# Two transformer blocks on one Trainium2 core: seven quarter products per weight tile in the first block's output products and in the second block's input product, with modulation weights brought as halves

## The reference

```
for l in range(2):                                       # first block
    shift, scale, gate = split(silu(c) @ w_ada[l] + b_ada[l], 3)
    h = rms_norm(x, norm_w[l]) * (1 + scale) + shift
    mix = three_mixers(h @ w_in[l])
    x = x + gate * (mix @ w_out[l])
sh1, sc1, ga1, sh2, sc2, ga2 = split(silu(c_2) @ w_mod + b_mod, 6)      # second block
px = (rms_norm(x, norm_mix) * (1 + sc1) + sh1) @ w_in_2
pc = (the same of ctx, with its own modulation) @ w_in_2
mix = mixers(px, pc)           # conv3 over tokens of the columns, wkv scans, short conv, Fourier
x = x + ga1 * (mix @ w_out_2)
x = x + ga2 * ((silu(h3 @ w_gate) * (h3 @ w_up)) @ w_down)
out = rms_norm(x, norm_final)
```

## Time and profile of the kernel before

| | before |
|---|---|
| runs | 3432.41, 3434.14, 3436.14 us |
| span of the profiled execution | 3419.8 us |
| its own time | not listed apart from the three runs |
| median of the runs less this span | 14.3 us |
| PE busy | 3148.4 us (92%) |
| DVE, ACT, POOL busy | 1497.6, 543.4, 900.9 us |
| mean granted TensorE clock | 0.963 |
| output products of layer 0 | 593.6 to 709.4 us of the span |
| output products of layer 1 | 1245.4 to 1372.1 us |
| second block's input product | 1379.0 to 1817.9 us |

### The profile page before, as it was taken

One profiled execution on the slowest core, in us unless ns is written; L12 is line 12 of the kernel. 1 busy time (PEld: TensorE's weight loads), 2 busy tenths in 40 slices (PEclk: granted clock), 3 DMA queues, 4 the chain that ended last, 5 costly groups with the idle time before them and its releaser, 6 DMA issues.

```text
span 3419.8 us, 67514 instructions
## 1 busy us (share of the span) xinstructions
PE 3148.4 (92%) x31278; PEld 2723.8 (80%) x31278; DVE 1497.6 (44%) x2300; ACT 543.4 (16%) x1011; POOL 900.9 (26%) x545
## 2 busy tenths in 40 slices
PE   5999999998999999999996888887899999999998
PEld 4877887877878888444785777677889999999998
DVE  4745365464447511333534666667334432113111
ACT  1012102020210211100002344333110000000001
POOL 1000000000000010000000121112447797777774
PEclk8998999998999999999997999999999999999999
DMA  7955387764336553333772000000436654444443
GB/s 275 409 219 197 133 328 280 307 247 172 124 136 255 200 194 123 148 148 141 264 296 112 8 9 10 7 7 6 159 126 232 237 217 162 167 170 161 161 163 109
DMA packets 52571, 582.97 MB, mean 170 GB/s; under 512 B 6931, under 2 KB 9297, under 8 KB 10433
## 3 DMA queue, kind: packets, MB, share of 16 engines
q1 hardware_dynamic: 34352, 465.06, 35.9%
q0 software_dynamic: 17936, 113.59, 8.6%
HBM read 576.52 MB, written 2.10 MB: 169 GB/s over the span
## 4 chain that ended last, share of the span: by engine, by line
PE 75%; DVE 10%; DMA 7%; ACT 3%; issue 3%; POOL 1%; SPq 0%; ACTq 0%; DVEq 0%; POOLq 0%
PE PS L1599 24%; PE PS L366 14%; PE PS L1548 10%; PE PS L664 6%; DMA ring<-in_w_second_dram 3%; DMA ring<-in_w_vec_dram 2%; PE PS L409 2%; PE PS L1767 1%; PE PS L1780 1%; PE PS L363 1%; DVE ring L201 1%; PE PS L1616 1%; DMA ring<-in_w_start_dram 1%; PE PS L1558 1%; PE PS L1812 1%
## 5 line engine op out<-in xcount | busy, mean ns | idle before, releaser
L366 PE MATMUL PS<-H,ring 128*128 128x256 f32 x2944 | 668.8, 386 | 7.0 <-ACT H L694 7.0
L366 PEld LDWEIGHTS PS<-H,ring 128*128 128x128 f32 x2944 | 562.1, 193 | 94.9 <-issue 17.6
L1548 PE MATMUL PS<-H,ring 128*128 128x256 f32 (+2 forms) x1344 | 403.1, 462 | 5.7 <-DMA ring<-in_w_second_dram 5.5
L1599 PE MATMUL PS<-H,ring 128*128 128x128 f32 x3424 | 404.0, 275 | 2.2 <-DMA ring<-in_w_second_dram 2.2
L1599 PEld LDWEIGHTS PS<-H,ring 128*128 128x128 f32 x3424 | 394.2, 192 | 3.0 <-DMA ring<-in_w_second_dram 2.6
L1548 PEld LDWEIGHTS PS<-H,ring 128*128 128x128 f32 (+1 forms) x1344 | 254.1, 190 | 155.0 <-issue 124.7
L2224 DVE TENSOR_TENSOR W<-W,PS 128x256 f32<-128x256 f32 x58 | 24.4, 421 | 679.9 <-ACT W L1925 679.8
L1599 PE MATMUL PS<-H,W 128*128 128x128 f32 x2624 | 316.5, 276 | 5.3 <-POOL W L1451 4.6
L1599 PEld LDWEIGHTS PS<-H,W 128*128 128x128 f32 x2624 | 305.3, 193 | 6.0 <-POOL W L1451 5.0
L319 POOL DMA_DIRECT2D ring<-in_w_vec_dram x75 | 39.8, 530 | 919.9 <-DVE ring L880 780.8
L1446 POOL TENSOR_TENSOR W<-ring 128x1024 f32<-128x1024 f32 (+1 forms) x74 | 179.6, 2427 | 264.6 <-PE PS L1599 147.9
(11 more groups left out here) (473 smaller groups left out, 4380.4 us busy)
## 6 DMA issues: line engine op xcount, KB each, us to landing
ring<-in_w_second_dram SPq DMA_DIRECT2D x121, 2048.0 KB, 7.7
ring<-in_w_first_dram SPq DMA_DIRECT2D x68, 2048.0 KB, 7.7
ring<-in_w_vec_dram POOLq DMA_DIRECT2D x75, 1024.0 KB, 7.6
ring<-in_w_start_dram SPq DMA_DIRECT2D x16, 2048.0 KB, 15.5
H<-in_w_vec_dram POOLq DMA_DIRECT2D x21, 1024.0 KB, 7.9
Pj<-in_w_aside_dram SPq DMA_DIRECT2D x8, 2048.0 KB, 11.2
ring<-in_w_second_dram SPq DMA_DIRECT2D x9, 1536.0 KB, 7.1
Pj<-in_x_dram SPq DMA_DIRECT2D x1, 2048.0 KB, 10.6
```

Of the source, the lines that this page charges most:

```text
L366: mm = pe.matmul(PS[:, t % 2, half * T:(half + 1) * T], ring[:, t % 2, k, half * P:(half + 1) * P], hT[:, k, :], start=(k == 0), stop=(k = ...
L1548: mm = pe.matmul(PS[0:cols, bank(q, half), 0:width], ring[:, q % RING].rearrange("p k n -> p (k n)")[:, k * 2 * cols + half * cols:k * 2 * ...
L1599: mm = pe.matmul(regions(bank2, r), w[:, k * P:(k + 1) * P], m[:, k, :], start=(first and k == 0 and r // 4 not in opened), stop=(last and ...
```

## The change

1. **First block's output products, tiles 1 to 7 of both layers.** Instead of 32 matmuls of 256 columns there are 7 regions of 8 matmuls of 128 columns, in the order 0, 1, 6, 4, 2, 3, 5. Region 4 needs POOL's first sum of weight quarters, made in place in the ring; 2, 3 and 5 need its second, third and fourth, in `S_out`, which exists once and may be written when the tile before has been multiplied. DVE makes four sums of the right side once per layer (`T_out`) after `mix_ready`. ACT copies region 0, DVE adds the others in four steps, then does the two gated additions to x.
2. **POOL's order in layer 0.** For tile n: the first sum, then the issues of 3, 3, 3, 3, 2, 1, 0 halves of modulation weights with their waits, then the other three sums. In layer 1 the first sum of tile 1 stands ahead of the small loads and the rest behind them.
3. **Second block's input product, tiles 1 to 7 and 10 to 21.** The same seven products, with 256 columns (tiles 1 to 7) or 128 (10 to 21), a copy on ACT, four additions on DVE, and DVE's convolution then reads the result from SBUF. Tiles 0, 8 and 9 stay plain. `S_in` exists once.
4. **Modulation weights.** The 24 whole tiles of `w_mod_2` beside it become 48 halves of 1 MB in the two halves of ring slot 2, the product's tiles use slots 0 and 1. SP issues tile q, then the halves that DVE sums in its step q-1 (4 for steps 0 to 8, 2 for 9 to 14, none after), each with a wait for the half two before it; only then tile q+1.
5. Twenty semaphores get second uses; the weights are laid out as quarters on the host.

```diff
-VEC0 = [0, 64, 96]
+VEC0 = [0, 64, 96, 144]
...
+OUT_VEC = [3, 3, 3, 3, 2, 2, 2]
...
+    T_out = blocks(Pj[:, 32:48, :]).rearrange("p (n k t) -> p n k t", n=4, t=P)
+    S_out = blocks(Pj[:, 48:60, :]).rearrange("p (n a) -> p n a", n=3)
+    c_out = [blocks(W[:, a:a + 2, :]).rearrange("p (r t) -> p r t", t=P) for a in (24, 26)]
...
+    def quarter1(t, n):
+
+        return ring[:, t % 2].rearrange("p k n -> p (k n)")[:, 1024 * n:1024 * n + 1024]
...
+    def out_sums(pool, l, n, begun):
+
+        t, sums = NIN + n, S("out_sum")
+        if begun:
+            pool.wait_ge(load[t % 2].sem, load[t % 2].at(l, 16 * (t // 2 + 1)))
+            sums.inc(pool.tensor_tensor(quarter1(t, 2), quarter1(t, 0), quarter1(t, 2), ALU.subtract))
+            return
+        pool.wait_ge(tiles_done.sem, tiles_done.at(l, t))
+        pool.wait_ge(sums.sem, sums.at(l, 4 * n - 3))
+        sums.inc(pool.tensor_tensor(S_out[:, 1], quarter1(t, 3), quarter1(t, 2), ALU.subtract))
+        pool.wait_ge(sums.sem, sums.at(l, 4 * n - 2))
+        sums.inc(pool.tensor_tensor(S_out[:, 0], S_out[:, 1], quarter1(t, 0), ALU.add))
+        sums.inc(pool.tensor_tensor(S_out[:, 2], quarter1(t, 1), S_out[:, 1], ALU.subtract))
...
+        def half(l, i):
+            pool.wait_ge(vec_done.sem, vec_done.start + (-1 if i < 2 else i - 2 if l == 0 else max(i - 1, VEC0[1])))
+            half_loaded[half_place(i)].inc(pool.dma_start(half_slot(i), A["w_vec"][i]), 16)
...
+            ahead = VEC0[1] - sum(OUT_VEC) + 3 if l == 0 else VEC0[2]
+            for i in range(VEC0[l], ahead):
+                half(l, i)
             if l < NL - 1:
+                pool.wait_ge(S("mix_ready").sem, S("mix_ready").at(l, 4))
+                for n in range(1, NOUT):
+                    out_sums(pool, l, n, True)
+                    for i in range(ahead, min(ahead + OUT_VEC[n - 1], VEC0[1])):
+                        half(l, i)
+                    ahead += OUT_VEC[n - 1]
+                    out_sums(pool, l, n, False)
...
+                    for k in range(KC):
+                        if half == 0 and k % 4 == 0:
+                            need(S("mix_ready"), k // 4 + 1)
+                        mm = pe.matmul(PS[:, 4 + half, 0:T], ring[:, t % 2, k, half * P:(half + 1) * P], hT[:, k, :],
+                                       start=(k == 0), stop=(k == KC - 1))
+            else:
+                plan = {0: (quarter1(t, 0), half_of(0, 0), 0), 1: (quarter1(t, 1), half_of(1, 0), 0), 6: (quarter1(t, 3), T_out[:, 3], 0),
+                        4: (quarter1(t, 2), T_out[:, 2], 1), 2: (S_out[:, 1], T_out[:, 1], 2), 3: (S_out[:, 0], T_out[:, 0], 3),
+                        5: (S_out[:, 2], half_of(1, 1), 4)}
+                opened = set()
+                for r in (0, 1, 6, 4, 2, 3, 5):
+                    w, m, after = plan[r]
+                    if r == 6:
+                        need(S("out_t"), 1)
+                    if after:
+                        need(S("out_sum"), 4 * (n - 1) + after)
+                    for k in range(8):
+                        mm = pe.matmul(out_regions(n, r), w[:, k * P:(k + 1) * P], m[:, k, :], start=(k == 0 and r // 4 not in opened),
+                                       stop=(k == 7), skip_group_check=True)
+                        opened.add(r // 4)
             tiles_done.inc(mm)
...
+
+        def out_first(n):
+
+            if n:
+                need(tiles_done, NIN + n + 1)
+                do(f(c_out[n % 2][:, 3, :], out_regions(n, 0), ACT.Copy), S("out_first"))
...
+        settle()
+        do(v.tensor_tensor(t2, half_of(1, 1), t1, ALU.subtract))
+        settle()
+        do(v.tensor_tensor(t4, half_of(1, 0), t2, ALU.subtract), S("out_t"))
         for n in range(NOUT):
             t = NIN + n
             need(tiles_done, t + 1)
+            if n:
+                c = c_out[n % 2]
+                need(S("out_first"), n)
+                do(v.tensor_tensor(c[:, 0:4:3, :], c[:, 3, :].unsqueeze(1).to_broadcast([P, 2, P]), out_regions(n, 1, 3), ALU.add))
+                settle()
+                do(v.tensor_tensor(c[:, 1:3, :], c[:, 3, :].unsqueeze(1).to_broadcast([P, 2, P]), out_regions(n, 3, 5), ALU.add))
+                settle()
+                do(v.tensor_tensor(c[:, 3, :], c[:, 2, :], out_regions(n, 3), ALU.add))
+                settle()
+                do(v.tensor_tensor(c[:, 1:3, :], c[:, 1:3, :], out_regions(n, 5, 7), ALU.add))
+                settle()
             for half in range(2):
                 k = 2 * n + half
-                ins = stt(xT[:, k, :], PS[:, 4 + 2 * (n % 2) + half, 0:T], mod[:, 32 + k:33 + k], xT[:, k, :], ALU.mult, ALU.add)
+                got = blocks(c)[:, half * T:half * T + T] if n else PS[:, 4 + half, 0:T]
+                ins = stt(xT[:, k, :], got, mod[:, 32 + k:33 + k], xT[:, k, :], ALU.mult, ALU.add)
                 if half:
                     evac[t % 2].inc(ins)
...
-NFIRST2 = NMOD1
-NVEC2 = 24
-NLATE2 = NMOD2 - NFIRST2 - NVEC2
+NLATE2 = 8
+BESIDE_TILE = [4] * 9 + [2] * 6 + [0] * 7
...
+    vec = [("w_mod_2", 0, TW * j, KC, TW) for j in range(NMOD2 - NLATE2, NMOD2)]
+    tiles = [("w_in_2", 0, c0, KC, 2 * LORA if c0 == WD0 else TW) for c0 in WIN2]
...
+NWIDE = 9
+SEVENS = Q_IN[1:NWIDE - 1] + Q_IN[NWIDE + 1:] + Q_OUT[1:] + Q_FF[1:] + Q_DN
+NSI = SEVENS.index(Q_OUT[1])
+SLOT = [q % 2 if q < NIN2 else (q - NIN2) % RING for q in range(len(SECOND))]
...
+    S_in = flat(W[:, 16:28, :]).rearrange("p (n a) -> p n a", n=3)
+    T_wide = [*(Pj[:, 32 + 8 * n:40 + 8 * n, :] for n in range(3)), W[:, 0:8, :]]
+    T_half = [h2[:, 4 * n:4 * n + 4, 0:T].rearrange("p k (b t) -> p k b t", t=P) for n in range(4)]
+    c_wide, c_half = Pj[:, 56:60, :], flat(Pj[:, 56:58, :]).rearrange("p (r t) -> p r t", t=P)
...
+        def halves(first, count):
+            for i in range(VEC0[2] + first, VEC0[2] + first + count):
+                sp.wait_ge(vec_done.sem, vec_done.at(NL, i - VEC0[2] - 1))
+                sp.dma_start(half_slot(i), A["w_vec"][i]).then_inc(half_loaded[half_place(i)].sem, 16)
...
+            before = BEFORE2[q]
+            if q < 2:
                 sp.wait_ge(tiles_done.sem, NL * tiles_done.per + tiles_done.start - (q == 0))
-                sp.wait_ge(vec_done.sem, vec_done.at(NL, 0))
-            elif q - RING in Q_VEC:
-                sp.wait_ge(vec_done.sem, summed(q - RING))
-            else:
-                sp.wait_ge(tiles_done.sem, multiplied(q - RING))
-            sp.dma_start(ring[:, q % RING].rearrange("p k n -> p (k n)")[:, 0:nk * wide], A["w_second"][q][:, 0:nk * wide]).then_inc(load[q % RING].sem, 16)
+            elif before in Q_VEC:
+                sp.wait_ge(vec_done.sem, summed(before))
+            elif before is not None:
+                sp.wait_ge(tiles_done.sem, multiplied(before))
+            sp.dma_start(ring[:, SLOT[q]].rearrange("p k n -> p (k n)")[:, 0:nk * wide], A["w_second"][q][:, 0:nk * wide]).then_inc(load[SLOT[q]].sem, 16)
+            if 0 < q < NIN2:
+                halves(sum(BESIDE_TILE[0:q - 1]), BESIDE_TILE[q - 1])
...
+        for n in range(1, NOUT):
+            if n > 1:
+                B["out_sums"](pool, NL - 1, n, True)
+            B["out_sums"](pool, NL - 1, n, False)
+        Sig.layers = kept
+
+        sums = S("ff_sum")
+        pool.wait_ge(S("h_scaled_2").sem, S("h_scaled_2").start + KC)
+        for n, q in enumerate(SEVENS[0:NSI]):
+            pool.wait_ge(load[SLOT[q]].sem, loaded(q))
+            sums.inc(pool.tensor_tensor(quarter(q, 2), quarter(q, 0), quarter(q, 2), ALU.subtract))
+            if n:
+                pool.wait_ge(tiles_done.sem, multiplied(SEVENS[n - 1]))
+            pool.wait_ge(sums.sem, sums.start + 4 * n + 1)
+            sums.inc(pool.tensor_tensor(S_in[:, 1], quarter(q, 3), quarter(q, 2), ALU.subtract))
+            pool.wait_ge(sums.sem, sums.start + 4 * n + 2)
+            sums.inc(pool.tensor_tensor(S_in[:, 0], S_in[:, 1], quarter(q, 0), ALU.add))
+            sums.inc(pool.tensor_tensor(S_in[:, 2], quarter(q, 1), S_in[:, 1], ALU.subtract))
...
+        def seven_in(q, n, wide, order):
+
+            m_, t = place[q], T_wide if wide else T_half
+            own, at = (side, lambda a, k: a[:, k, :]) if wide else (side_half, lambda a, k: a[:, k // 2, k % 2, :])
+            plan = {0: (quarter(q, 0), own(0, 0), 0), 1: (quarter(q, 1), own(1, 0), 0), 6: (quarter(q, 3), t[3], 0),
+                    4: (quarter(q, 2), t[2], 1), 2: (S_in[:, 1], t[1], 2), 3: (S_in[:, 0], t[0], 3), 5: (S_in[:, 2], own(1, 1), 4)}
+            opened, per = set(), 2 if wide else 4
+            for r in order:
+                w, m, after = plan[r]
+                if r == order[3 if wide else 2]:
+                    need(S("in_t"), 1 if wide else 2)
+                if after:
+                    need(S("ff_sum"), 4 * m_ + after)
...
+            elif n == NWIDE:
+                product(q, lambda k: h2[:, k, T:2 * T], T)
             else:
```

(39 more changed lines are left out.)

154 lines of the change are left out of this document (95 added, 59 removed).

## The result

The changed kernel takes 3450.89 us (median of 6 runs, 3442.95 to 3462.14), the kernel before, beside it on the same chip, 3433.86 (6 runs, 3428.41 to 3441.33). The ratio is 1.0053, 95% interval 1.0039 to 1.0066: slower by 17 us, where 3442.5 and "slower", by 8.4 us, were forecast. The profiled execution has a span of 3441.2 us and took 3442.95, so 1.8 us lie around a span in this series.

The account below looks back on a forecast made before the run. PE was taken to bound the kernel, with a matmul under way for 92% of the span. Layer 0 +31.1, layer 1 -3.1 and second block -19.6 gave +8.4, so 3442.5 us, range 3415 to 3460.

Parts of the forecast that it names:

- The forecast case: Whole kernel: all three stage sums of the sign forecast, slower by 8.4 us at 3442.5; chance 0.50, own range 3433 to 3452.
- Layer 0, +31.1 forecast: Layer 0's output products: PE waits for POOL's sums behind halves' issues that DVE releases; +31.1 us, bounds +24 and +36.
- The clock's price: PE's slowdown after idle time: 1.8 us after 2.29 idle, 2.6 after 3.90, 2.9 after 7.04.
- The tail: End of layer 0's output products: last x 2.1 us later, next condition vector holding ACT's silu about 1 us; +3.
- Layer 1, -3.1 forecast: Layer 1's output products: seven shorter tiles gain 9.1 us, less tile 1, tail and late DVE; -3.1, bounds -8 and 0.
- Second block, -19.6 forecast: Second block's input product: shorter tiles, partly lost to gated loads and engine turns; 402 us, saving 19.6, bounds 7 and 58.
- The base: Profiled span of 3419.8 us plus 14.3 to the runs' median, the rest of the kernel keeping its instructions.
- Full mutual exclusion: Rival: at the port shared by DVE and POOL, short convolution operations push sums; about 11 us more, 3453 us; chance 0.20.
- The first rival: Second block's input product runs without waits, loads in time and turns rare: 3404 us in full, 3427 in part; chance 0.15.
- The third: Rival: layer 0 has no wait because the halves' issues come off early; -6 instead of +31, 3405 us; chance 0.10.
- the fourth: Rival: 256-column regions with new weight blocks do not shorten tiles; 27.5 us per wide tile, 15 more, 3457; chance 0.05.

Follow-up runs that it names:

- the run with layer 0 plain: Changed kernel with layer 0's output products back in the form of before, without sums or ScalarE copies: 3418.99 us, ratio 0.9956.
- the two moves: Second block: tile loads ahead of each batch's later half, halves of tiles 9 to 14 moved to 15 to 20; with layer 0's halves spread 3380.15 us.
- the run with three moves: Changed kernel with layer 0's 18 halves earlier, second-block loads ahead of each batch's later half, halves of tiles 9 to 14 at 15 to 20: 3432.94 us.
- the run with early loads: Changed kernel with SyncE issuing the second block's next tile load ahead of the later half of each batch: 3438.72 us, ratio 1.0013.

## Why the prediction was right, point by point

The forecast case, layer 0's wait outweighing what the second block gains, is what happened, and the run with layer 0 plain shows the loss to be there. The change in time is twice the forecast: 17 us slower for 8.4. The changed stages add 9.2 us in the first pair of profiles and 11.2 by the means (721.5 - 710.3), against +8.4. That closeness is partly luck: the three stages were off by +2.4, +2.4 and -4.0 us, which nearly cancel. By the spans the miss is 13.0 us (3441.2 for 3428.2), and 12.2 of them lie outside the changed stages.

- **Layer 0, +31.1 forecast, +33.5 measured** (159.2 - 125.7). Tiles: +26.0 (141.7 us from tile 0's start to tile 7's end where it was 115.8) against 28.1. Tiles 2 to 4 were forecast at 21.1 and came 20.9, 20.65 and 20.56 us apart, with idle of 5.01, 4.87 and 4.86 for 5.1. Tile 1 idled 3.65 for 3.6. The clock's price was put too high: the two regions behind the wait took 6.14, not 6.3, and less in tile 1 (5.57). The tail was the missized term, +7.5 for +3: the last x came late by the 2.1 us forecast, but the condition vector, issued behind tile 7's sums, held ScalarE for 5.3 us and not 1.
- **Layer 1, -3.1 forecast, -0.7 measured.** Both ends came as forecast, +5.0 for +2.1 and +2.9: PE waited 4.82 us behind tile 7 for DVE, whose step 6 came late as described, and from tile 7's end to the input product it is 11.83 us where it was 6.83. Tile 7 with the squares took 13.4. The missized term is tile 1, +3.4 against a tile that waits for nothing (16.8 us with the squares, for 13.4), where +1.0 had been put down. Timelines of POOL and PE:

```profile
1287.29 2.35 POOL L318 TENSOR_TENSOR ring<-ring 128x1024 f32<-128x1024 f32 x1 [2.37 <-DMA ring<-in_w_first_dram]
...
1303.64 2.05 PE L729 MATMUL PS<-Pj 128*128 128x128 f32 x16 [2.02 <-POOL Pj L322]
```

  The first sum, ahead of the small loads, itself waits 2.37 us for the tile's weights, a wait that the forecast did not have. So the last small load was issued 20.8 us behind tile 0's start and not 18.6, and PE waited for all three sums behind it, 2.02, 0.37 and 0.26 us, and not for the last alone.
- **Second block, -19.6 forecast, -24.1 measured** from tile 1 on (397.4 for 402); tile 0 took 0.5 more than before, which makes -23.6 for the stage. The mechanism was as described, a load behind a half behind a row product: tile 10 idled 8.93 for 8.5, the end 2.65 for 3. The wide tiles averaged 25.0, not 25.4: waits of 0.9 to 1.5 us, four of them, cost nothing behind them (7.17 for 32 records where 7.07 is plain), where up to 1.8 had been put down. Tiles 8 and 9 had no wait and took 41.5 for 43.3. Tiles 11 to 15 took 77.6 for 79, but the nearness is luck: the forecast had DVE and POOL take turns in every tile, and what made it up were two waits for loads (5.63 and 2.23) and two for sums in tile 15.
- **The base.** "The rest of the kernel keeps its instructions" was taken as no change, against one profile that proved the fastest of four. The instructions are the same, and by the medians their time is some 6 us longer, 6 to 12 over all eight profiles of changed kernels; the cause is open.
- **Rivals.** Full mutual exclusion was half of the truth, and not where the rival had put it: in layer 0, once the queue order is mended, it keeps 15 us in the tiles (121.6 against the 106.6 that are left without row products), and the condition vector keeps 10 more in the tail (21.8 against 12.05). In the second block it makes DVE late and through it the halves, not the sums. The first rival's sum, no wait in the second block, is nearly had by the two moves: 399.5 against 451.6, 52 us saved where 58 is the bound without any wait. The third, no wait in layer 0, falls by PE's 5.01 us there, and the fourth, wide regions that are not shorter, by tile 1 of the second block: 24.18 us from its start to tile 2's, for the 24.17 forecast.

## What to carry to other kernels

Before work is given to a second engine, add up both engines' time on what they share, over one tile: three row products of 2.28 and four sums of 2.36 are 16.3 us under a tile of 13.4; with the sums put first the tiles came 16.8 us apart on average. When such a wait is removed, look for the next limit of the same size, and move the work to where its engine waits for the bottleneck, one piece per wait. Ahead of a load should stand only what the load needs. And take the base of a sum from the median of the runs, or from several profiles: the same kernel's untouched stages differed by 15 us from one profile to the next.

## What the runs showed of the hardware

**Short operations of DVE lose whole sums of POOL, POOL loses part of a short operation.** In the run with three moves, tiles 10 to 14 have convolutions beside POOL's sums and nothing else. DVE's timeline, a pair beside sums and a pair (1702.78) without:

```profile
1702.78 1.00 DVE L2317 SCALAR_TENSOR_TENSOR Pj<-Pj,rope 128x255 f32<-128x255 f32 x2
...
1709.97 5.01 DVE L2317 SCALAR_TENSOR_TENSOR Pj<-Pj,rope 128x255 f32<-128x255 f32 x2
```

and the two sums of POOL that held them:

```profile
1709.87 2.35 POOL L1549 TENSOR_TENSOR W<-W,ring 128x1024 f32<-128x1024 f32 x1
1712.18 2.53 POOL L1550 TENSOR_TENSOR W<-ring,W 128x1024 f32<-128x1024 f32 x1
```

DVE lost 4.0 us to POOL, POOL 0.2 to DVE. One of these operations takes 0.50 us alone; one of 128x510 takes 0.77, and in wide tiles 4 to 7 of the changed kernel the two sums that meet such a pair took 2.67 to 2.80 for 2.35, so they lost 0.3 to 0.45. With row products both lose about two: 4.4 for 2.28, 4.39 for 2.35. The Trainium skill (SBUF — State Buffer, Who interferes with whom) has the whole instruction block the other engine, from either side. The trace agrees for long ones and for POOL against DVE; of a short one of DVE, POOL lost a part that grows with its length, not the full length.

**An operation with one input waits too.** In the changed kernel the convolution's first step reads SBUF and not PSUM; the timeline of DVE in a wide tile, without and beside sums of POOL:

```profile
1481.26 0.48 DVE L2390 TENSOR_SCALAR Pj<-Pj,rope 128x512 f32<-128x512 f32 x1
...
1495.54 2.16 DVE L2390 TENSOR_SCALAR Pj<-Pj,rope 128x512 f32<-128x512 f32 x1
```

It is faster than from PSUM (0.48 where the earlier trace rows has 0.75), and beside POOL it is 2.16. The same section of the Trainium skill says of this operation that it can take both ports and then contends; the trace agrees.

**Idle time of PE has no fixed price.** Behind a wait of 1.47 us 32 records took 7.17 where 7.07 is plain, behind one of 2.02 us 16 took 2.05 where 1.95 is; behind 2.30 us 16 took 3.07, and behind 5.01 us 32 took 6.14 for 3.74. In narrow tiles 64 records, 7.31 plain, took 7.41 behind 2.23 us and 9.04 behind 2.49 us (the run with early loads, granted clock 0.54 in the first 3 us). The windows of the changed kernel (length, busy times, then the granted clock) show the first of these at full clock and the last at half of it, the 1.2 of 2.4 GHz:

```profile
639.70:642.70 3.00, 2.97 (x14) 2.97 (x15) 0.00 (x0) 0.00 (x0) 2.95 (x2) 0.50 0.88 347
...
1518.40:1525.60 7.20, 7.17 (x33) 6.34 (x34) 7.02 (x6) 0.00 (x0) 6.92 (x3) 1.00 0.54 223
```

So a load that comes a microsecond late costs that microsecond and no more here, which is why the wide tiles lost less than forecast.
